# Recurrence of a decoder step: work of the next unit moved into the inverse's tail, products regrouped, and rotary transposes shared by two pages

## The reference

```python
def one_seq(args):                                   # per sample sequence
    c_all = concatenate([cache_c[m, pt], cn])        # 16 pages x 128 rows x 256 latent
    kr_all = concatenate([cache_kr[m, pt], krn])     # 16 pages x 128 rows x 64 rotary
    k = mla_keys(c_all, kr_all, w_uk, g_kn)
    p = softmax(q @ k * scale); o = p @ c_all @ w_uv

def wkv_step(state, inp):                            # per head, 64 x 64 state, per token
    r, w, k, v, a, b = inp                           # w = decay, a = -kk, b = kk * rate
    sa = einsum('bhij,bhj->bhi', state, a)
    state = state * w[:, :, None, :] + sa[..., None] * b[:, :, None, :] + v[..., None] * k[:, :, None, :]
    return state, einsum('bhij,bhj->bhi', state, r)
# then per head: y minus its mean, over the root of its variance, plus a bonus, times a gate
```

## Time and profile before

| | us |
|---|---|
| three runs | 3055.57, 3061.04, 3063.80 |
| profiled execution, its own time | 3059.15 |
| its span | 3057.2 |
| TensorE busy | 2900.6 |
| VectorE, ScalarE, GpSimd busy | 2111.7, 1349.4, 714.0 |
| attention over the cache, about | 631 to 1137 |
| recurrence, about | 2200 to 2603 |

### The profile page before, as it was taken

One profiled execution on the slowest core, in us unless ns is written; L12 is line 12 of the kernel. 1 busy time (PEld: TensorE's weight loads), 2 busy tenths in 40 slices (PEclk: granted clock), 3 DMA queues, 4 the chain that ended last, 5 costly groups with the idle time before them and its releaser, 6 DMA issues.

```text
span 3057.2 us, 69119 instructions
## 1 busy us (share of the span) xinstructions
PE 2900.6 (95%) x28799; PEld 2779.1 (91%) x28799; DVE 2111.7 (69%) x2724; ACT 1349.4 (44%) x2410; POOL 714.0 (23%) x557
## 2 busy tenths in 40 slices
PE   8999999999999999999999999999878887999999
PEld 8999997589999988999999999999866776999999
DVE  6977865656666663788786977873446666488976
ACT  4433434445555552344344433433445554334432
POOL 1322210410000002123220322341035553211321
PEclk9999999999999999999999999999989999999999
DMA  3222212111111102232222223312100001222322
GB/s 118 96 98 87 93 65 75 29 45 36 36 36 49 51 34 69 70 97 91 89 83 81 94 89 97 97 56 83 63 3 19 19 19 42 83 79 87 95 85 87
DMA packets 78973, 208.21 MB, mean 68 GB/s; under 512 B 25505, under 2 KB 42274, under 8 KB 63714
## 3 DMA queue, kind: packets, MB, share of 16 engines
q1 hardware_dynamic: 78690, 204.16, 21.0%
HBM read 198.63 MB, written 5.49 MB: 67 GB/s over the span
## 4 chain that ended last, share of the span: by engine, by line
PE 85%; DVE 7%; ACT 4%; issue 3%; DMA 0%; POOL 0%; DVEq 0%; SPq 0%; POOLq 0%; ACTq 0%
PE PS L469 25%; PE PS L285 22%; PE PS L1589 11%; PE PS L2187 5%; PE PS L2479 5%; PE PS L642 5%; PE PS L1570 1%; PE PS L1616 1%; PE PS L2167 1%; DVE WL L269 1%; DVE DOWN L771 1%; DVE WL L435 1%; PE PS L1232 1%; PE PS L1213 1%; PE PS L1214 1%
## 5 line engine op out<-in xcount | busy, mean ns | idle before, releaser
L408 POOL TENSOR_TENSOR WLF<-RAW 128x512 f32<-128x512 f32 x72 | 94.0, 1305 | 979.2 <-PE PS L285 656.8
L264 ACT ACTIVATE WH<-RAW 128x1536 fp32r<-128x1536 f32 (+3 forms) x112 | 171.4, 1530 | 323.2 <-PE PS L285 195.6
L269 DVE TENSOR_TENSOR WL<-RAW,WH 128x1536 fp32r<-128x1536 f32 (+3 forms) x113 | 217.9, 1929 | 119.1 <-ACT WH L264 119.1
L1589 PE MATMUL PS<-UKMH,CTH 128*128 128x384 f32 (+1 forms) x768 | 269.3, 351 | 0.4 <-POOL RQL L1532 0.4
L469 PE MATMUL PS<-XH,WH 128*128 128x288 f32 x864 | 255.1, 295 | 8.3 <-DVE M L510 8.3
L1663 DVE TENSOR_REDUCE SS<-SQ 128x4 f32<-128x512 f32 x256 | 173.5, 685 | 119.9 <-ACT SQ L1648 118.0
L469 PE MATMUL PS<-XH,WL 128*128 128x288 f32 x864 | 255.2, 295 | 0.0
L469 PE MATMUL PS<-XL,WH 128*128 128x288 f32 x864 | 254.8, 295 | 0.0
L1589 PE MATMUL PS<-UKMH,CTL 128*128 128x384 f32 (+1 forms) x768 | 252.6, 329 | 0.0
L1648 ACT ACTIVATE SQ<-PS 128x384 f32<-128x384 f32 (+1 forms) x384 | 172.3, 455 | 132.5 <-PE PS L1589 132.5
L285 PE MATMUL PS<-HH,WH 128*128 128x288 f32 x1056 | 225.3, 295 | 1.2 <-DVE WL L269 1.2
(11 more groups left out here) (636 smaller groups left out, 9010.3 us busy)
## 6 DMA issues: line engine op xcount, KB each, us to landing
RAW<-in_w SPq DMA_DIRECT2D x113, 1024.0 KB, 4.9
RAW<-in_w SPq DMA_DIRECT2D x48, 768.0 KB, 5.0
ROWS<-in_cache_c SPq DMA_DIRECT2D x128, 128.0 KB, 2.0
RAW<-in_w SPq DMA_DIRECT2D x16, 512.0 KB, 4.4
ROWS<-in_cache_kr SPq DMA_DIRECT2D x128, 32.0 KB, 1.8
RAW<-in_w SPq DMA_DIRECT2D x8, 384.0 KB, 3.2
X<-in_x SPq DMA_DIRECT2D x4, 576.0 KB, 7.7
out_y<-X SPq DMA_DIRECT2D x8, 288.0 KB, 2.3
```

The lines of the kernel that those rows point to most:

```text
L264: act.activation(WH[n % 2][:, 0:cols], RAW[n % 2][:, 0:cols], ACT.Copy).then_inc(rounded, 1)
L269: dve.tensor_tensor(WL[n % 2][:, 0:cols], RAW[n % 2][:, 0:cols], WH[n % 2][:, 0:cols].bitcast(F32), ALU.subtract).then_inc(item_split, 1)
L1589: mm = pe.matmul(out[:, 0:c1 - c0], c[u][:, x], w, start=t == 0, stop=t == 5)
```

## The change

*Attention.* The rotary key rows get tiles of their own (KRS). One transpose turns the rotary rows of two pages: the even page lands on partitions 0 to 63, the odd one on 64 to 127, and `page_dve` puts the low part in whichever half is free. QL's rotary rows 0 to 63, before zero, now hold the low part of the query.

*Recurrence.* Unit f + 1's rates, scan, decays, BT, K2, KTI, AR0 are made in iteration f, behind the state steps. R0 and AXT come from one set of 128-column products of XA with RV and ATOK side by side (RA, two banks), half of it beside each Gram block. Every crossing block stands beside a straight one. Banks and several tiles' places change with it. The variance of unit b - 1 is summed at the head of the next iteration; root, reciprocals, `scaled`, `shifted` and `gate` follow there.

```diff
-        for k, c in enumerate((0, P, ROW - P)):
-            mm = pe.transpose(bank(6)[:, k * P:(k + 1) * P], row[:, p, c:c + P], IDENT)
+        for k in range(KV_T):
+            mm = pe.transpose(bank(6)[:, k * P:(k + 1) * P], row[:, p, k * P:(k + 1) * P], IDENT)
+        if p % 2 == 0:
+            mm = pe.transpose(bank(6)[:, KV:KV + P], KRS[s % 2][:, p:p + 2, :].rearrange("p a r -> p (a r)"), IDENT)
...
+    RA = m.at("RA", BLOCKS[35], [NB, 2, CH])
+    RV, ATOK = RA[:, :, 0, :], RA[:, :, 1, :]
...
+            def corrections(c):
+                for r, out in zip(HEADS, HEADS[::-1]):
+                    mm = pe.matmul(RA_PS[out, c], XA[r, c, :], RA[r, c], start=True, stop=True)
+                return mm
...
-                products(5, at(XA), at(RV), across=chain).then_inc(q["r0"], 1)
...
-                    products(6, at(XA), at(ATOK), across=True).then_inc(q["axt"], 1)
...
+            for c in range(NB):
+                if front:
+                    x = products(0, at(BT), at(AR0), (c,))
+                if chain and c % 2:
+                    mm = corrections(c // 2)
...
+            if p:
+                wait("y_norm", y_at(p, "sq_lo"))
+                head_sums(5, YH, YL).then_inc(q["y_norm"], 1)
...
+                wait("gamc", b)
+                if p:
+                    wait("y_norm", y_at(p, "yroot"))
+            state(1)
...
+                if more:
+                    rates(f + 1)
...
+                if chain:
+                    wait("y_norm", y_at(b, "y_lo"))
+                    head_sums(5, YH, YL).then_inc(q["y_norm"], 1)
```

ScalarE, end of an iteration (new order):

```diff
             if prompt:
+                off_diagonal(f, 1)
+            if more:
+                sigmoids(f + 1)
+            if front:
+                wait("rv", n)
+                act.activation(RV, cells(3), ACT.Copy).then_inc(q["rvc"], 1)
+            if prompt:
+                off_diagonal(f, 2)
+            if more:
+                decays(f + 1)
+                key_factor(f + 1)
...
             if chain:
                 wait("y", 2 * b)
...
                 if p:
                     wait("y_norm", y_at(p, "yg"))
                 act.activation(flat(Y1), bank(7), ACT.Copy).then_inc(q["y_norm"], 1)
```

VectorE and GpSimd, end of an iteration (new order):

```diff
+            if p:
+                inverse_part(p, 0)
+            if prompt:
+                inverse_sum(1)
+            if more:
+                sums_of_rates(f + 1)
+            if prompt:
+                inverse_turned(1)
+            if p:
+                inverse_part(p, 1)
+            if front:
+                wait("bon_mm", n)
+                dve.tensor_tensor(unit(VT_, f), cells(3), unit(VT_, f), ALU.mult).then_inc(q["bv"], 1)
+            if p:
+                inverse_part(p, 2)
+                inverse_part(p, 3)
+                scaled(p)
+                shifted(p)
+            if more:
+                decayed_direction(f + 1)
...
+            if more:
+                decayed_keys(f + 1)
+            if p:
                 gate(p)
+            if more:
+                keys_in_place(f + 1)
+            if chain and not last:
+                wait("y_norm", y_at(b, "yc"))
+                pool.tensor_tensor(flat(YL), flat(Y1), flat(YH).bitcast(F32), ALU.subtract).then_inc(q["y_norm"], 1)
```

## The result

The changed kernel is slower, by 0.7 to 0.8%. In two comparisons its median was 3082.61 and 3082.57 us, beside 3061.65 and 3057.27 us for the kernel before; the ratios are 1.0068 (95% interval 1.0048 to 1.0087) and 1.0083 (1.0068 to 1.0097). The forecast was 3058 us with a range up to 3075. The profiled execution took 3082.91 us.

A forecast was written before the change was run, and what follows sets the result against it. TensorE, busy 2900.6 of 3057.2 us, was taken as the bound, with instruction supply pacing the recurrence's dense stretches. Terms -6.4 - 7.5 - 4.6 + 6.1 + 9.3 = -3.1 us gave 3058 us, 8-in-10 range 3036 to 3075.

The forecast's parts named there:

- the steady unit: Recurrence from unit 2 to 8: 41.2 us a unit against 40.0, +6.1 us over six intervals.
- The tail chain: Steady unit, from the second off-diagonal product through all engines to the mean sum: 16.2 us with handoffs.
- Two blocks at that rate: Steady unit after TensorE's idle time: two blocks at half clock add 1.4 us, half hidden in a stall, leaving 0.7.
- Rival 2: Recurrence: longer idle before the mean sum, low clock over five or six blocks a unit; +15 us, 3073; chance 0.17.
- the four numbers: Whole-program times: forecast 3058, packets cost nothing 3032, more low clock 3073, change doesn't do what it says 3070 us.
- the 3.2 us for supply: Steady unit's head: instruction packets make the second off-diagonal product 3.2 us late, between 1.6 and 3.9.
- Rival 1: Recurrence: supply and clock cost nothing more than now, six intervals fall by 17.5 us; 3032 us; chance 0.30.
- Units 0 and 1: Recurrence start: distance between their first Gram blocks falls from 37.3 to 29.8 us, -7.5 (-12 to -3).
- Unit 1 to 2: First XT interval, with no mean to wait for: 34.0 against 38.6 us, -4.6 (-8 to 0).
- The last unit: End of the recurrence: corrections start later, YLZ and the final mean move back, +9.3 us (+3 to +12).
- Transposes: Attention over cached pages: 64 of 384 transposes go at 0.10 us each, 6.4 us gained.
- PEclk digits below 9 all through the recurrence: Sign in the profile page's TensorE clock slices that the forecast is wrong and rival 2 holds.

The follow-up runs named there:

- e3_busy: Changed kernel with fourteen short, useless matmuls ahead of each mean sum to keep TensorE busy; ratio to the kernel before 1.0063, median 3073.82 us.
- e7: Changed kernel with VectorE's reciprocals, scaling and shift moved ahead of the second turned sum in the middle iterations; ratio to the kernel before 1.0053.
- e5: Changed kernel, same instructions reordered on VectorE, GpSimd and ScalarE; ratios to the kernel before 0.9988 and 0.9986, medians 3050.32 and 3052.47 us.
- Experiment 4: The run e7: changed kernel with only VectorE's order altered in the middle iterations; ratio to the kernel before 1.0053.
- e4_supply: Kernel before with 1024 additional matmuls that depend on nothing at the start of the recurrence; ran once, 3094.91 us.
- e9_unpaired: Changed kernel with all fifteen paired loops split, each pair's blocks issued one after the other; ratio to the kernel before 1.0128.
- experiment 6: The run e5, done twice: changed kernel with all queues reordered; ratios to the kernel before 0.9988 and 0.9986, medians 3050.32 and 3052.47 us.
- e8_last_unit: Changed kernel with the four reciprocals, scaling and shift ahead of the S0 sum in the last iteration alone; ratio to the kernel before 1.0053.

## Why the prediction was wrong, step by step

**The failed term is the steady unit,** 41.2 us forecast (246.0 / 6 = 41.0 with the lighter one), 44.5 measured (266.7 / 6), and in it the tail. The forecast cut a unit at its first Gram block and at its second off-diagonal product. The same cuts in the profiles, us, mean of five steady units:

| | to the off-diagonal product | from it to the next Gram block |
|---|---|---|
| forecast | 24.0, and 0.7 for the clock | 16.2 + 0.3 |
| changed kernel, two profiles | 25.0, 25.8 | 20.0, 19.6 |
| with busy matmuls (e3_busy) | 23.6 | 19.1 |
| VectorE's order alone (e7) | 25.0 | 19.7 |
| reordered (e5), two profiles | 24.5, 23.7 | 16.0, 16.7 |

- *The tail chain was walked without two of its links.* Take the unit of the rows above, whose product starts at 2388.67 and whose next Gram block starts at 2408.39, 19.7 us. First, "gate on GpSimd 1.27" was put right behind the shift; in the trace it waits from 2401.81 to 2402.96 for BT, 1.15 us. The forecast had named the queue's K2, and not BT ahead of the gate. Second, supply: "lateness of supply in the tail costs only 0.3, as ScalarE's exponentials start from that product". A packet ended inside that very product (the row says issue, 1.42 us), so the copy to ZZ came at 2391.47:

```profile
2388.67 0.28 PE L2490 MATMUL PS<-XA,OF 64*64 64x64 f32 x4
...
2390.37 0.27 PE L2490 MATMUL PS<-RT,BT 64*64 64x64 f32 x2 [1.42 <-issue]
...
2391.47 0.60 ACT L2898 ACTIVATE ZZ<-PS 128x512 f32<-128x512 f32 x1 [1.96 <-PE PS L2490]
2392.08 1.28 ACT L2869 ACT_TABLE_LOAD   x1
```

Product to end of the copy is 3.4 us, not 1.8: +1.6. The XT sum waited 0.76 us for TensorE, which had another such stall of 0.60: +0.7. With 0.4 for a mean sum at half clock that is some 3.8 of extra against 3.2 found (19.7 less 16.5); the scaling, 0.75 instead of 1.33, gives most of the rest back. So the term of 16.5 was mis-sized by 3 to 3.5 us in each of six intervals, some 20 us: the 20.7 of this row, out of 26.9 for the whole program. Where the order is changed so that BT no longer stands there (e5), the tail is 16.0 and 16.7.
- *The path was the wrong one as well.* The forecast led it over VectorE's reciprocals, scaling and shift. Experiment 4 has these done 11.5 us before the gate starts, and the tail keeps its 19.7. What ends last runs along TensorE's own queue to the third off-diagonal product, stalls of 1.42, 0.60 and 0.72 us included, then over its ZZ copy (2399.06), a table load and an exponential (done at 2401.60) to BT, the gate, y's copy and YL. How the 3.2 us of excess split between the stalls (2.7 us in this unit, where 0.3 was allowed for) and the queue behind BT was not measured.
- *Half clock.* "Two blocks at that rate, of which half falls into the stall: 0.7" was too small. The half clock covered the mean sum, both Gram blocks, the gates and the variance sum, 6 us of work. With the clock kept up the head took 23.6 instead of 25.0 to 25.8 us, in one profile. But the head came out only 0.3 to 1.1 us above the forecast's 24.7, so other parts of that walk were too dear by as much. Rival 2 saw rightly a longer idle time and a half clock over more blocks, and its 3073 is the nearest of the four numbers. But it blamed the clock for what was mostly the longer chain, so that number is near by luck: the first profile of e5 has a clock of 0.91 over its intervals, the changed kernel 0.90, and they last 281.2 and 305.2 us.
- *Supply.* The head came out near its forecast, though the 3.2 us for supply in it was not measured by itself, and e4_supply and e9_unpaired hold up the reading that a unit's instructions, not its array time, bound the dense part. Rival 1 (packets cost nothing, 3032) is out. The rule of the Trainium skill ("Runtime: NRT & Kernel Launch", instruction fetch mechanics) that fetching is mostly hidden does not fit these dense small matmuls: 1.66 and 1.93 us of each 4 were not hidden.
- *Units 0 and 1:* -5.2 against -7.5, inside its ends. *Unit 1 to 2:* -0.3 against -4.6, just inside them too. TensorE is idle for 4.51 us before that Gram block (2273.63), and the clock is 0.50 behind it; the forecast had no half clock in this unit. The profile calls the wait issue, but the MK1 copy ends at 2273.11, and as in experiment 6 the block follows it. The tail of this unit takes 13.8 us, where 12 was forecast; the rest is in the head, and how that splits was not measured.
- *The last unit:* +10.3 against +9.3. The forecast is a later start of 3.5 and then 5.8 for what stands ahead of YLZ. Measured from the XT copy, the S0 sum is 6.0 us later (36.9, before 30.9) and YLZ loses another 5.3 behind it. The four reciprocals are part of it, as forecast (e8_last_unit moves them and gets 3.3 us back). "Who is late next there is VectorE, alone" is wrong: YLZ waits 1.78 us for ScalarE, behind the gate on GpSimd.
- *Transposes:* 320 records as forecast, and a wait for CTH of 21.8 us over 33 pages, as before:

```profile
L1574 PE MATMUL PS<-CONST,ROWS x256: 270/273/332, 627.6 to 1122.7; 128*128 128x128 f32 x128
...
  DVE CTH L1665: 21.8, 33
```

The stretch itself gave 7.8 us (4 to 6 in the kernel with this part alone), where 6.4 was forecast. What the forecast took for granted is that a gain in an earlier stage is kept by the later ones: the whole program keeps 2 to 4 us of it when the part stands alone.

Of what was named as showing the steps right, 320 records, the wait for YL, and the last YLZ behind the reciprocals were there; XT copies 41 us apart were not. The sign "PEclk digits below 9 all through the recurrence" pointed to rival 2, and the page shows it in four of six slices; but the kernel of experiment 6, which is 30 us faster, has four such digits too in its first profile, so the sign doesn't tell the two apart.

## What to carry to other kernels

When work of the next unit is moved into the tail of this one, write down for each in-order queue what it now passes, down to the instruction that waits for another engine: here one BT that waits for an exponential, ahead of the gate of y, held up TensorE in each steady unit, and moving VectorE's work alone left the tail of such a unit at 19.7 us. The same instructions in another order were worth 30 us, more than the 18.5 that the forecast's three gains add up to. Removing a wait uncovers the next one: a wait of 6.4 us was worth 3.2, as the next one was already running behind it. A tail that passes through TensorE products can pay for the supply of instructions at each product it waits for, since a packet's end can fall inside a product (1.42, 0.60 and 0.72 us in the unit above); count that along the chain, not only along TensorE's own work.

## What the runs showed of the hardware

- Small fp32 matmuls that depend on nothing came in groups of 128, 256 instructions with their loads, 3.75 to 4.02 us apart, while a group's work took 2.1 to 2.4 us; alternating the blocks of all fifteen paired loops gained 12 us in the whole program.
- In one unit of the changed kernel the granted clock fell to 0.50 within a wait of 6.4 us, stayed there for the first 6 us of work, and was at 1.00 in the window of 2414.
- On GpSimd the last gate took 3.24 us while VectorE split the weights, and 1.27 us where it was done before that split (e8_last_unit).
- Work taken out of an earlier stage, or put in ahead, moved the recurrence's intervals from 279 to 284 to 286 us with the same matmuls. The cause is open.
